# Sparse attention of the second block: norms, angle tables and key rotation issued between the input product's tiles, index scores and attention queries reordered

## The chip, the cores and the metric

One core of one Trainium2 chip runs the whole program in one launch. The metric is the device time of one execution in microseconds (us). TensorE does matrix products and transposes (PE, and PEld for its weight loads), VectorE (DVE) and ScalarE (ACT) do element work, GpSimd (POOL) does element work and issues some DMAs, SyncE (SP) issues the large weight loads.

## The reference, cut to what matters

Two models of two layers each run one after the other on 256 tokens of width 2048. The change lies in the first layer of the second model. There one product `h = xn @ even_w_in` gives all inputs of a sparse attention (`dsa_mixer`) and of a recurrent mixer (`rwkv7_mixer`), which shifts its part by one token and blends it.

```python
def dsa_mixer(h, cos_a, sin_a, cos_i, sin_i, cq_norm, ckv_norm, kidx_norm, w_uq, w_uk, w_uv, w_qidx):
    c_q, c_kv, k_rope, k_idx, w_idx = split_cols(h, [512, 256, 32, 64, 16])
    c_q = rms_norm(c_q, cq_norm)
    c_kv = rms_norm(c_kv, ckv_norm)
    k_rope = apply_partial_rope(k_rope, cos_a, sin_a, 32)
    q = einsum('bsr,rhd->bshd', c_q, w_uq)                 # 8 heads of 128
    q_rope = apply_partial_rope(q[..., :32], ...)
    q_lat = einsum('bshd,rhd->bshr', q[..., 32:], w_uk)
    q_idx = apply_partial_rope(einsum('bsr,rhd->bshd', c_q, w_qidx), ...)   # 16 heads of 64
    k_idx = apply_partial_rope(rms_norm(k_idx, kidx_norm), ...)
    # per block of 128 queries:
    score = einsum('bqh,bqhs->bqs', w_idx, relu(q_idx . k_idx))
    sel = top_k(where(allowed, score, -inf), 64)
    # softmax of (q_lat . c_kv + q_rope . k_rope) over the selected keys, times c_kv, times w_uv
hm = h + (token_shift(h) - h) * mu                         # rwkv7_mixer's columns
```

## The kernel before, in words

**Products.** A weight slab of 2 MB is loaded into a ring of three by SyncE (L258 to L273). Every tile (128 output channels) of a product takes half of one. ScalarE rounds the tile's weights to fp32r in two halves (`act_feed`, L295), VectorE subtracts to get the remainder of the first half (`dve_feed`, L311), GpSimd that of the second half (`pool_feed`, L329). `pe_tile` (L336) then runs 16 pairs of matmuls, L349 and L350. VectorE adds the tile's two halves out of PSUM (L362) and multiplies by the norm (L559). Pieces of a tile go into one of two buffers, so a tile's feed may begin when the tile two before it is done, and `ahead` lets every engine feed one tile ahead.

**The input product** (`pe_evin`, `act_evin`, `dve_evin`) has 35 tiles, n = 0 to 34. Tiles 0 to 7 are the sparse attention's own (`cq`, `ckv`, `kid`, `kro`, the last with the index weights in it). Tiles 8 to 34 belong to the recurrent mixer: after sum and norm VectorE makes three more instructions on each, L1618 (times mu), L1620 (subtract) and L1622 (add the shifted row). In rounds 1 to 16 VectorE also scales one block of the residual stream (L1603). VectorE's order in a round is: feed the next tile, L1603, sum and norm of tile n, L1618, L1620, L1622. ScalarE in a round only feeds.

**The sparse attention** (`pe_dsa`, `act_dsa`, `dve_dsa`, `pool_dsa`) starts when tile 34 is done. In order: GpSimd loads the constants (L1636, L1637); VectorE computes two angle tables, with ScalarE's sines (L1651 to L1677); TensorE turns the index weights (L1723); three norms one after the other, each of squares (L437, L447), a sum by TensorE (L1711), a root (L439), a reciprocal (L449) and a product (L482); the rotation of the two keys (TensorE L1690, VectorE L1697, L1698, L1700); a transpose of `ckv` (L1736); eight tiles of index queries and then eight of attention queries (L1748, copied out by ScalarE L1865), each rotated; eight index products (L1764) with two ReLUs each (ScalarE L1872) and 32 accumulations (VectorE L1920); the selection `dve_select` (L1936), first all of the first 128 queries, then all of the others; and a loop of 13 rounds over the eight heads (L1767 to L1806): latent queries L1778, scores L1790 and L1791, masking and maximum (L625, L628, L630), exponential (L642), share (L650, L652), transpose (L1816), values (L1829), output (L1805) and copy (L1933). GpSimd's loads for the recurrent mixer come behind: L1997 and L1998 after tile 34, L2001 after the last scores. The recurrent mixer waits for the last head.

**What orders it.** There is no planner for this part. Every engine has its list of instructions written out by hand, and waits on counting semaphores: `K.dve.of(key)` is the count at which the instruction recorded under that key is done. `K.dve.now()` is the count of the instruction just before, so that wait makes an instruction wait for its predecessor. PSUM banks are taken in turn.

## Time and profile before

| | |
|---|---|
| runs shown | 4569.15, 4564.98, 4549.57 us; median 4564.98 |
| the profiled execution | 4556.82 us, of which 4555.5 us span |
| mean granted TensorE clock | 0.931 |
| PE, DVE, ACT, POOL busy | 91%, 61%, 40%, 34% |

The profiled execution lies between the runs. Its span is from the first to the last instruction; 1.3 us lie around it. All times in the rows below are us from the start of the span.

### The profile page before, as it was taken

To read this page: it belongs to the slowest core of one execution; us is meant where nothing else is said; L and a number is where in the kernel's file an instruction comes from. 1 tells how busy PE (TensorE), PEld (TensorE's weight loads), DVE (VectorE), ACT (ScalarE), POOL (GpSimd) and SP (SyncE) were. 2 spreads that over 40 slices of the span, in tenths; PEclk is the share of its full clock that TensorE was granted. 3 is DMA by queue.
4 is the path that set the end of the run, shared out by engine and by line. 5 is a ranking of instruction groups with operands and counts; after the bars stand their busy time and mean duration, and the time that the engine had idled before them with its cause. 6 is when DMAs were issued, how large, how long until landed. Compare 5 with 4: busy or idle time off the path is not lost.

```text
span 4555.5 us, 58299 instructions
## 1 busy us (share of the span) xinstructions
PE 4151.7 (91%) x24034; PEld 3456.0 (76%) x24034; DVE 2778.9 (61%) x4036; ACT 1819.2 (40%) x2818; POOL 1526.8 (34%) x710
## 2 busy tenths in 40 slices
PE   5898999999999857877899999999799998999998
PEld 3786887778788745666677888888676887888887
DVE  0436635863688865554768464468997577554557
ACT  1435434543553323211444343344364454343334
POOL 0332432333234300000333444444465442444443
PEclk8999999999999978777899999999876999999999
DMA  8653665345444400000444554555200543545543
GB/s 362 259 208 135 251 247 190 145 178 222 167 148 166 181 19 15 1 1 1 167 165 169 185 189 183 196 189 186 111 1 27 198 183 130 187 183 187 196 180 139
DMA packets 53481, 711.35 MB, mean 156 GB/s; under 512 B 5952, under 2 KB 8128, under 8 KB 10848
## 3 DMA queue, kind: packets, MB, share of 16 engines
q1 hardware_dynamic: 47664, 684.15, 40.1%
q0 software_dynamic: 3488, 21.37, 1.3%
q8 instruction: 190, 3.11, 0.3%
q10 hardware_dynamic: 2064, 2.10, 0.1%
q14 instruction: 75, 0.61, 0.0%
HBM read 705.50 MB, written 2.10 MB: 155 GB/s over the span
## 4 chain that ended last, share of the span: by engine, by line
PE 73%; DVE 18%; ACT 4%; DMA 2%; issue 2%; POOL 0%; DVEq 0%; ACTq 0%; POOLq 0%; SPq 0%
PE ps L349 37%; PE ps L350 19%; DVE pieces L311 3%; DMA ring<-in_ada 2%; PE ps L758 2%; ACT pieces L295 1%; PE ps L2198 1%; DVE r L1139 1%; DVE opb L538 1%; PE ps L2992 1%; DVE scr L503 1%; PE ps L2993 1%; DVE opa L538 1%; PE ps L1748 1%; PE ps L2222 1%
## 5 line engine op out<-in xcount | busy, mean ns | idle before, releaser
L349 PE MATMUL ps<-opa,pieces 128*128 128x512 f32 x6192 | 2245.8, 406 | 73.7 <-DVE pieces L311 48.4
L329 POOL TENSOR_TENSOR pieces<-ring,pieces 128x1024 fp32r<-128x1024 f32 x539 | 1356.4, 2517 | 2617.3 <-ACT pieces L295 2581.6
L350 PE MATMUL ps<-opa,pieces 128*128 128x256 f32 x6192 | 1740.2, 281 | 0.0
L295 ACT ACTIVATE pieces<-ring 128x1024 fp32r<-128x1024 f32 (+1 forms) x1110 | 1098.6, 1036 | 919.6 <-PE ps L350 912.9
L349 PEld LDWEIGHTS ps<-opa,pieces 128*128 128x128 f32 x6192 | 1171.0, 189 | 373.1 <-issue 64.3
L350 PEld LDWEIGHTS ps<-opa,pieces 128*128 128x128 f32 x6192 | 1177.2, 190 | 8.0 <-issue 4.8
L349 PE MATMUL ps<-opb,pieces 128*128 128x512 f32 x2560 | 910.4, 397 | 24.1 <-DVE pieces L311 19.6
L311 DVE TENSOR_TENSOR pieces<-ring,pieces 128x1024 fp32r<-128x1024 f32 (+1 forms) x571 | 732.4, 1283 | 263.3 <-ACT pieces L295 261.4
L350 PE MATMUL ps<-opb,pieces 128*128 128x256 f32 x2560 | 726.4, 284 | 0.0
L349 PEld LDWEIGHTS ps<-opb,pieces 128*128 128x128 f32 x2560 | 483.8, 189 | 144.9 <-DVE x L391 20.2
L350 PEld LDWEIGHTS ps<-opb,pieces 128*128 128x128 f32 x2560 | 484.3, 189 | 0.1
L389 DVE TENSOR_TENSOR x<-ps,x 128x256 f32<-128x256 f32 x192 | 81.2, 423 | 319.0 <-PE ps L350 319.0
L362 DVE TENSOR_REDUCE scr<-ps 128x256 f32<-128x512 f32 x203 | 140.1, 690 | 177.1 <-PE ps L350 176.7
L408 ACT ACTIVATE opb<-scr 128x256 fp32r<-128x256 f32 x129 | 53.9, 418 | 445.2 <-DVE scr L2715 444.7
L503 DVE TENSOR_TENSOR scr<-scr 128x256 f32<-128x256 f32 x195 | 140.8, 737 | 18.5 <-ACT scr L494 15.1
L559 DVE TENSOR_TENSOR scr<-scr,rstd 128x256 f32<-128x256 f32 x136 | 125.6, 924 | 4.6
L758 PE MATMUL ps<-ring,ada 128*32 128x256 f32 x1536 | 105.6, 422 | 24.9 <-DMA ring<-in_ada 24.9
L362 DVE TENSOR_REDUCE m<-ps 128x256 f32<-128x512 f32 x48 | 33.2, 691 | 112.6 <-PE ps L350 112.6
L758 PEld LDWEIGHTS ps<-ring,ada 128*32 128x32 f32 x1536 | 48.5, 118 | 65.6 <-DMA ring<-in_ada 26.7
L413 DVE TENSOR_TENSOR opb<-scr,opb 128x256 fp32r<-128x256 f32 x129 | 54.9, 425 | 62.5 <-ACT opb L408 62.5
L391 DVE TENSOR_TENSOR x<-ps,x 128x256 f32<-128x256 f32 x192 | 81.5, 424 | 6.6
L1032 ACT ACTIVATE scr<-m 128x256 f32<-128x256 f32 x48 | 20.0, 418 | 162.1 <-DVE m L362 162.1
(467 smaller groups left out, 4222.3 us busy)
## 6 DMA issues: line engine op xcount, KB each, us to landing
ring<-in_up SPq DMA_DIRECT2D x64, 2048.0 KB, 7.8
ring<-in_down SPq DMA_DIRECT2D x64, 2048.0 KB, 7.8
ring<-in_win SPq DMA_DIRECT2D x56, 2048.0 KB, 8.2
ring<-in_ada SPq DMA_DIRECT2D x48, 2048.0 KB, 12.1
ring<-in_wout SPq DMA_DIRECT2D x24, 2048.0 KB, 8.1
ring<-in_evin SPq DMA_DIRECT2D x18, 2048.0 KB, 7.9
ring<-in_evout SPq DMA_DIRECT2D x8, 2048.0 KB, 7.9
ring<-in_xkv SPq DMA_DIRECT2D x8, 2048.0 KB, 7.9
```

The costliest lines, as they stand in the source:

```text
L295: a.do.activation(K.parts_of(p)[0][:, s, :], w[:, s, :], ACT.Copy).then_inc(*K.hi.up((p, h)))
L311: v.do.tensor_tensor(lo[:, s, :], w[:, s, :], hi[:, s, :].bitcast(F), ALU.subtract).then_inc(*K.lo.up(p))
L329: g.do.tensor_tensor(lo[:, s, :], w[:, s, :], hi[:, s, :].bitcast(F), ALU.subtract).then_inc(*K.lo2.up(p))
L349: pe.do.matmul(b[:, 0:512], hi[:, k, :], op[:, 512 * k:512 * k + 512], start=i == 0, stop=False)
L350: t = pe.do.matmul(b[:, 0:256], lo[:, k, :], half(op, 0, k), start=False, stop=i == kt - 1)
L362: return K.v.do.tensor_reduce(out, b, AX.X, ALU.add)
L389: v.do.tensor_tensor(x, b[:, 0:256], x, ALU.add).then_inc(*K.dve.up())
L391: v.do.tensor_tensor(x, b[:, 256:512], x, ALU.add).then_inc(*K.dve.up(key))
L503: v.do.tensor_tensor(K.acc[z], K.acc[z], K.sqr[z][k % 2], ALU.add).then_inc(*K.dve.up((*key, "acc", k)))
L538: K.v.do.scalar_tensor_tensor(out=half(op, 1, k), in0=src, scalar=gain, in1=half(op, 0, k).bitcast(F), op0=ALU.mult, op1=ALU.subtract).the ...
L559: return v.do.tensor_tensor(out, out, rstd[0:out.shape[0]], ALU.mult)
L758: t = pe.do.matmul(b[q:q + 32, 0:256], K.sc[:, 2 * k:2 * k + 32], w[:, k, :], start=k < 4, stop=k >= 12)
```

## The change

It does these things:

1. `act_evin` and `dve_evin`: for tiles 8 to 34, L1618 and L1620 are replaced by one ScalarE instruction, tile times (1 - mu), one round later, and VectorE's shifted add (before L1622) follows a round later too, after the next feed. Two small instructions make `omu` = 1 - mu.
2. New functions `pe_dsa_ahead`, `act_dsa_ahead`, `dve_dsa_ahead` are called once in every round. They issue the three norms (rounds 8 to 17), the turn of the index weights (19, 20), the angle tables (19 to 29) and the two key rotations (30 to 33).
3. `pool_dsa` goes in front of the feeds of tiles 18 to 34, waits for the last L1603, and issues three DMAs in place of two. The constants lie in the upper half of the `mix` buffer.
4. `pe_dsa` and the others: index queries, their rotation, index products and scores run in one loop of 11 rounds. The attention queries come behind it, which on TensorE is while VectorE selects. Their rotation is done two heads ahead inside the loop over heads.
5. `dve_select` takes its steps for both query blocks in turn, and waits for the same block's step before, no longer for the instruction just before.

```diff
 def act_evin(K):
-    for n in range(35):
-        act_feed(K, ahead(K, p + n))
+    for n in range(36):
+        if n < 35:
+            act_feed(K, ahead(K, p + n))
...
+        if n > 8:
+            d, h, mu, om = shifted(K, n - 1)
+            a.wait_ge(*K.dve.of(("evn", n - 1)))
+            a.do.activation(d, h, ACT.Identity, scale=om).then_inc(*K.act.up(("evd", n - 1)))
+        act_dsa_ahead(K, n)
 def dve_evin(K):
+    for a, w, name in ((0, 24, "mu"), (24, 3, "mul")):
+        v.do.tensor_scalar(K.omu[:, a:a + w], K.col(name), -1.0, 1.0, ALU.mult, ALU.add).then_inc(*K.dve.up())
...
+        if n > 8:
+            d, h, mu, om = shifted(K, n - 1)
+            v.wait_ge(*K.act.of(("evd", n - 1)))
+            v.do.scalar_tensor_tensor(out=d[:, 1:256], in0=h[:, 0:255], scalar=mu, in1=d[:, 1:256], op0=ALU.mult,
+                                      op1=ALU.add).then_inc(*K.dve.up(("ev", n - 1)))
+        dve_dsa_ahead(K, n)
...
-        v.do.tensor_scalar(d, h, mu, None, ALU.mult).then_inc(*K.dve.up())
-        v.do.tensor_tensor(d, h, d, ALU.subtract).then_inc(*K.dve.up())
-        v.do.scalar_tensor_tensor(out=d[:, 1:256], in0=h[:, 0:255], scalar=mu, in1=d[:, 1:256], op0=ALU.mult,
-                                  op1=ALU.add).then_inc(*K.dve.up(("ev", n)))
+            d = shifted(K, n)[1]
+            if n > 9:
+                v.wait_ge(*K.dve.of(("ev", n - 2)))
+        dve_normed(K, p + n, d, K.rr, ("evs", n)).then_inc(*K.dve.up(("evn", n)))
 def pool_dsa(K):
-    g.wait_ge(*K.tile.of(K.first["evin"] + 34))
-    g.do.dma_start(K.dc, K.D["dsac"]).then_inc(*K.load["dsac"].up("dsac", 16))
+    g.wait_ge(*K.dve.of(("nf", "y", 15)))
+    g.do.dma_start(K.iota, K.D["dsac"][:, 0:256]).then_inc(*K.load["io5"].up("iota", 16))
+    g.do.dma_start(K.dc, K.D["dsac"][:, 256:1028]).then_inc(*K.load["dsac"].up("dsac", 16))
     g.do.dma_start(K.sfi[:, 0:1].bitcast(I32), K.D["sf"]).then_inc(*K.load["sf"].up("sf", 16))
+def pe_dsa_ahead(K, n):
+    if n in (9, 11, 13):
+        i = (n - 9) // 2
+        key, src, _, _ = dsa_norms(K)[i]
...
+        pe.wait_ge(*K.act.of((key, "sq")))
+        for k in range(len(src)):
+            t = pe.do.matmul(b[:, 0:256], K.ones, K.sqd[k], start=k == 0, stop=k == len(src) - 1)
+    if n == 19:
...
+            t = pe.do.transpose(b[:, P * i:P * i + P], K.kro[:, P * i:P * i + P], K.ident)
+    if n in (30, 31):
...
+        pe.do.matmul(b[:, 0:256], perm, buf, start=True, stop=True).then_inc(*K.prod.up(key))
+def act_dsa_ahead(K, n):
+    if n in (10, 12, 14):
+        a.do.activation(K.rsd[i], K.bank[key][:, 0:256], ACT.Sqrt, bias=K.eps[1e-5], scale=1.0 / width).then_inc(*K.act.up((key, "std")))
+    if n in (8, 10, 12):
+        for k, x in enumerate(src):
+            a.do.activation(K.sqd[k], x, ACT.Square).then_inc(*K.act.up((key, "sq")))
+    if n == 20:
+        a.do.activation(K.wix, ...)
+        a.do.activation(K.kro, K.kro, ACT.Copy, scale=K.inv[:, 2:3]).then_inc(*K.act.up("kro"))
+    if n in (23, 28):
+        a.do.activation(dsa_tables(K)[2 * i + 1], K.an, ACT.Sin).then_inc(*K.act.up())
+        a.do.activation(K.turns, K.an, ACT.Sin, scale=0.5).then_inc(*K.act.up(("sine", i)))
+def dve_dsa_ahead(K, n):
+    if n in (11, 14, 16):
+        v.do.reciprocal(K.rsd[i], K.rsd[i]).then_inc(*K.dve.up((dsa_norms(K)[i][0], "rstd")))
+    if n in (12, 13, 15, 17):
+        for k in ks:
+            v.do.scalar_tensor_tensor(out=src[k], in0=src[k], scalar=gain(k), in1=K.rsd[i], ...)
...
+    # angle tables: the eleven instructions of each, one or two a round, from rounds 19 and 24
+    if n in (32, 33):
+        v.do.tensor_tensor(an, K.bank[key][:, 0:256], sin, ALU.mult).then_inc(*K.dve.up((*key, "sin")))
+        v.do.tensor_tensor(buf, buf, cos, ALU.mult).then_inc(*K.dve.up())
+        v.wait_ge(*K.dve.now())
+        v.do.tensor_tensor(buf, buf, an, ALU.add).then_inc(*K.dve.up((*key, "done")))
 def pe_dsa(K):
     pe.wait_ge(*K.dve.of(("ev", 34)))
+    pe.wait_ge(*K.dve.of(("rkr", "done")))
...
+    for n in range(11):
+        if n < 8:
+            pe_dsa_queries(K, "qidx", n)
+        if 0 <= n - 1 < 8:
+            pe_rope2(K, ("r", "qidx", n - 1), K.permI, K.qi[:, n - 1, :], K.act, ("qidx", n - 1))
+        if 0 <= n - 3 < 8:
+            pe_dsa_index(K, n - 3)
+    for n in range(8):
+        pe_dsa_queries(K, "uq", n)
+    for n in range(2):
+        uq_rope(n)
...
+        if i + 2 < 8:
+            uq_rope(i + 2)
 def dve_dsa(K):
+    for n in range(11):
+        if n < 8:
+            dve_rope2(K, ("r", "qidx", n), K.qi[:, n, :], cosI, sinI, n)
+        for m in range(2 * n - 6, 2 * n - 4) if n >= 3 else ():
+            v.wait_ge(*K.act.of(("idx", m // 2, m % 2)))
+            v.wait_ge(*K.dve.now())
+            for qt in range(2):
+                v.do.scalar_tensor_tensor(out=K.SC[:, qt, :], ...).then_inc(*K.dve.up(("score", m)))
     dve_select(K)
+    for n in range(2):
+        uq_rope(n)
...
+        if i + 2 < 8:
+            uq_rope(i + 2)
 def pool_program(K):
     pool_block1(K)
+    pool_feed(K, K.first["evin"] + 17)
+    pool_dsa(K)
     pool_feed(K, K.first["evin"] + 34)
-    pool_dsa(K)
```

## Rows read from the trace of the kernel before

**Rows 1.** The page: busy time of the engines, and shares of the chain that ended last.
```profile
PE 4151.7 (91%) x24034; PEld 3456.0 (76%) x24034; DVE 2778.9 (61%) x4036; ACT 1819.2 (40%) x2818; POOL 1526.8 (34%) x710
...
PE 73%; DVE 18%; ACT 4%; DMA 2%; issue 2%; POOL 0%; DVEq 0%; ACTq 0%; POOLq 0%; SPq 0%
```
**Rows 2.** Windows: stretch, its length, busy us (instructions) by engine, granted clock, DMA.
```profile
1387.60:1420.90 33.30, 33.30 (x194) 29.36 (x193) 29.13 (x25) 12.09 (x13) 14.87 (x6) 1.00 0.43 163
1420.90:1475.60 54.70, 52.39 (x288) 43.63 (x286) 53.17 (x63) 18.05 (x19) 22.89 (x9) 1.00 0.51 189
1475.60:1577.10 101.50, 98.29 (x544) 82.94 (x544) 93.14 (x103) 33.43 (x33) 40.27 (x16) 1.00 0.51 187
1577.10:1612.00 34.90, 10.20 (x23) 6.49 (x24) 19.49 (x40) 6.07 (x14) 2.14 (x4) 0.53 0.17 53
1612.00:1648.00 36.00, 35.92 (x163) 30.74 (x161) 18.28 (x48) 6.74 (x17) 0.00 (x0) 0.98 0.16 59
...
1668.20:1691.50 23.30, 0.00 (x0) 0.00 (x0) 21.62 (x69) 0.00 (x0) 0.00 (x0) 0.50 0.00 0
1691.50:1744.70 53.20, 51.98 (x248) 45.10 (x248) 26.81 (x88) 24.52 (x66) 0.54 (x1) 0.96 0.08 30
```
**Rows 3.** Timeline of VectorE and GpSimd in the input product: start, us, instruction.
```profile
1416.39 1.22 DVE L311 TENSOR_TENSOR pieces<-ring,pieces 128x1024 fp32r<-128x1024 f32 x1
1417.41 2.48 POOL L329 TENSOR_TENSOR pieces<-ring,pieces 128x1024 fp32r<-128x1024 f32 x1 [2.98 <-ACT pieces L295]
1417.52 2.64 DVE L1603 SCALAR_TENSOR_TENSOR x<-x,cols,rstd 128x256 f32<-128x256 f32 x1
...
1477.16 0.42 DVE L1620 TENSOR_TENSOR even<-scr,even 128x256 f32<-128x256 f32 x1
1477.62 0.48 DVE L1622 SCALAR_TENSOR_TENSOR even<-scr,cols,even 128x255 f32<-128x255 f32 x1
1477.74 2.62 POOL L329 TENSOR_TENSOR pieces<-ring,pieces 128x1024 fp32r<-128x1024 f32 x1 [3.53 <-ACT pieces L295]
1478.02 3.42 DVE L311 TENSOR_TENSOR pieces<-ring,pieces 128x1024 fp32r<-128x1024 f32 x1
```
**Rows 4.** Timeline behind the last tile: sum of tile 34, constants, norms.
```profile
1577.07 0.68 DVE L362 TENSOR_REDUCE scr<-ps 32x256 f32<-32x512 f32 x1 [3.63 <-PE ps L350]
1577.33 0.55 POOL L1636 DMA_DIRECT2D dsa<-in_dsac  x1 [7.41 <-PE ps L350]
1579.05 0.47 DVE L1622 SCALAR_TENSOR_TENSOR even<-scr,cols,even 32x255 f32<-32x255 f32 x1
1602.20 1.75 DVE L449 RECIPROCAL rstd<-rstd 128x256 f32<-128x256 f32 x1 [2.78 <-ACT rstd L439]
```
**Rows 5.** Timeline of the queries, index products and scores.
```profile
1612.25 4.20 PE L1748 MATMUL ps<-even,ring 128*128 128x256 f32 x16
1618.87 1.89 PE L1748 MATMUL ps<-even,ring 128*128 128x256 f32 x8
1619.07 0.42 DVE L1697 TENSOR_TENSOR dsa<-ps,dsa 128x256 f32<-128x256 f32 x1 [0.94 <-PE ps L1690]
1619.42 0.41 DVE L1698 TENSOR_TENSOR dsa<-dsa 128x256 f32<-128x256 f32 x1
1619.87 0.42 DVE L1700 TENSOR_TENSOR dsa<-dsa 128x256 f32<-128x256 f32 x1
1621.03 1.89 PE L1748 MATMUL ps<-even,ring 128*128 128x256 f32 x8
1648.08 5.55 PE L1764 MATMUL ps<-even,dsa 64*128 64x256 f32 x48
1650.56 17.64 DVE L1920 SCALAR_TENSOR_TENSOR dsa<-scr,dsa 128x256 f32<-128x256 f32 x32
```
**Rows 6.** Timeline of the first heads.
```profile
1691.51 1.09 ACT L1881 ACTIVATE dsa<-ps 128x512 f32<-128x512 f32 x2 [26.00 <-DVE dsa L1967]
1692.25 2.05 PE L1790 MATMUL ps<-even,dsa 128*128 128x256 f32 x4 [32.06 <-ACT dsa L1881]
```

More of the change, by code:

```diff
@@ L1700, in dve_rope2, with pe_dsa_queries, pe_dsa_index @@
     v.do.tensor_tensor(buf, buf, t, ALU.add).then_inc(*K.dve.up((*key, "done")))
[L1703 removed]
+def pe_dsa_queries(K, name, n):
     pe = K.pe
[L1706 to L1712 removed]
+    ap, landed = K.slab_at(K.raw[name])
+    w = r3(ap, 4)
+    pe.wait_ge(*landed)
+    pe.wait_ge(*K.dve.of(("ncq", "y", 3)))
+    b, was = K.wide.take(K.act, (name, n))
+    K.bank[name, n] = b
+    pe.wait_ge(*was)
+    for k in range(4):
+        t = pe.do.matmul(b[:, 0:256], w[:, k, P * n:P * n + P], K.cq[:, k, :], start=k == 0, stop=k == 3)
+    t.then_inc(*K.prod.up(("slab", name) if n == 7 else (name, n)))
+def pe_dsa_index(K, i):
+    pe = K.pe
+    pe.wait_ge(*K.dve.of(("r", "qidx", i, "done")))
+    pe.wait_ge(*K.dve.of(("rki", "done")))
+    bb = []
+    for par in range(2):
+        b, was = K.wide.take(K.act, ("idx", i, par))
+        K.bank["idx", i, par] = b
+        pe.wait_ge(*was)
+        bb.append(b)
+    for par in range(2):
+        for qt in range(2):
+            t = pe.do.matmul(bb[par][:, 256 * qt:256 * qt + 256], K.qi[64 * par:64 * par + 64, i, qt * P:qt * P + P],
+                             K.kid[64 * par:64 * par + 64, :], start=True, stop=True)
+    t.then_inc(*K.prod.up(("idx", i)))
 def pe_dsa(K):
@@ L1787, in pe_dsa @@
                 pe.wait_ge(*K.act.of(("lat", n)))
-                pe.wait_ge(*K.dve.of(("rkr", "done")))
                 for c in range(2):
@@ new lines, in dve_select, with of, at, done @@
+    v = K.v
+    def of(qt):
+        return K.SC[:, qt, :], K.m8[:, qt, :], *(K.scr[:, 1536 + 1024 * qt + 256 * i:1792 + 1024 * qt + 256 * i] for i in range(4))
+    def at(key, qt):
+        v.wait_ge(*K.dve.of(("sel", key, qt)))
+    def done(t, key, qt):
+        t.then_inc(*K.dve.up(("sel", key, qt)))
+    both = range(2)
+    v.wait_ge(*K.dve.now())
+    for qt in both:
+        sc, m8, w, gt, eq, cum = of(qt)
+        done(v.do.tensor_tensor(sc, sc, K.allow[:, qt, :], ALU.add), "sum", qt)
@@ new lines, in dve_select @@
+    for qt in both:
+        sc, m8, w, gt, eq, cum = of(qt)
+        at("sum", qt)
+        done(v.do.tensor_copy(w, sc), ("w", 0), qt)
+    for r in range(8):
+        for qt in both:
+            sc, m8, w, gt, eq, cum = of(qt)
+            at(("w", r), qt)
+            done(v.do.max(m8[:, 0:8], w), ("m", r), qt)
+        for qt in both if r < 7 else ():
+            sc, m8, w, gt, eq, cum = of(qt)
+            at(("m", r), qt)
+            done(v.do.match_replace(w, m8[:, 0:8], w, -3.3e38), ("w", r + 1), qt)
@@ new lines, in dve_select @@
+    for qt in both:
+        sc, m8, w, gt, eq, cum = of(qt)
+        th = m8[:, 7:8]
+        at(("m", 7), qt)
+        done(v.do.tensor_scalar(gt, sc, th, 0.0, ALU.is_gt, ALU.add, accum_out=m8[:, 8:9]), "gt", qt)
+        done(v.do.tensor_scalar(eq, sc, th, None, ALU.is_equal), "eq", qt)
+        done(v.do.memset(w, 1.0), "one", qt)
+    for qt in both:
+        sc, m8, w, gt, eq, cum = of(qt)
+        at("one", qt)
+        done(v.do.tensor_tensor_scan(cum, w, eq, 0.0, ALU.mult, ALU.add), "cum", qt)
+        done(v.do.tensor_scalar(m8[:, 9:10], m8[:, 8:9], -1.0, 64.0, ALU.mult, ALU.add), "left", qt)
@@ new lines, in dve_select @@
+    for qt in both:
+        sc, m8, w, gt, eq, cum = of(qt)
+        at("left", qt)
+        done(v.do.tensor_scalar(cum, cum, m8[:, 9:10], None, ALU.is_le), "le", qt)
+    for qt in both:
+        sc, m8, w, gt, eq, cum = of(qt)
+        at("le", qt)
+        done(v.do.tensor_tensor(eq, eq, cum, ALU.mult), "take", qt)
+    for qt in both:
+        sc, m8, w, gt, eq, cum = of(qt)
+        at("take", qt)
+        done(v.do.tensor_tensor(gt, gt, eq, ALU.add), "all", qt)
+    for qt in both:
+        sc, m8, w, gt, eq, cum = of(qt)
+        at("all", qt)
```

288 lines of the change are left out of this document (119 added, 169 removed).

## The prediction

> **What bounds it now.** I read the page first. TensorE is busy for 91% of the span and carries 73% of the chain that ended last, VectorE 18% [rows 1]. So only stretches in which TensorE stands still, or works in small pieces behind a chain, can give much. The windows show where they lie [rows 2]. In the input product TensorE is busy nearly throughout at full clock (98.3 of 101.5 us in its last 17 tiles). Then come 34.9 us with 10.2 us of its work at a granted clock of 0.53, most of it at the lower level of 1.2 GHz: the constants, tables, norms and key rotations. Queries, rotations and index products fill it again until 1648, but then it waits for scores, and for the selection's 23.3 us it does nothing. The loop over heads is TensorE's own (52.0 of 53.2 us).
>
> **1. The work in front of the first query.** Tile 34's sum starts at 1577.07 and the first query matmul at 1612.25: 35.2 us [rows 4, 5]. After the change, what is left there is tile 34's own tail. Today it ends with L1622 at 1579.05 + 0.47 = 1579.5 [rows 4]; ScalarE takes over one of its steps and VectorE loses two, which I put at no difference. Behind it TensorE has the transposes of `ckv`, four of about 0.26 us (estimate from the 0.216 us of a query's record, below), say 1.1 us with starting up: the first query at 1580.6, 3.5 us behind the sum. **Gain 31.7 us.** The clock before that point was full and the pause is 2.2 us; the pauses of the 34.9 us window are longer, so whether it drops here no row says. If the first queries run at 1.2 GHz, 1.7 us more each: 0 to 4 us, I take 0.
>
> **2. Index queries and scores.** Today queries, index products and scores follow each other, 1612.25 to 1668.20 = 56.0 us. In the new loop a steady round has on TensorE four query matmuls and a rotation, 2.16 us (1618.87 to 1621.03), and an index product, 5.55/48 x 8 records = 0.93 us: 3.1 us [rows 5]. VectorE has a rotation, from 1619.07 to 1619.87 + 0.42 = 1.22 us, and four accumulations; today's 32 take 17.64 us, 0.55 each, since every one waits for the one before. The new ones wait once per pair. A pair without a wait starts 0.35 us apart (1619.07, 1619.42), one with it 0.45 (1619.42, 1619.87); so a pair of 0.48 us instructions takes about 0.93 and the round 1.22 + 1.86 = 3.1 us [rows 5]. ScalarE has a copy and two ReLUs, under 1.7 us by L1881's 1.09 for two of the same width [rows 6]. So the round is 3.1 us with the two engines level. TensorE's rounds 0 to 2 take 1.73 + 2 x 2.16, round 3 takes 3.1, and rotation 3 is 2.16 into round 4: 1591.9. From there VectorE has five rounds of 3.1 and three of 1.86: 1613.0. The stretch 1580.6 to 1613.0 is 32.4 us. **Gain 23.6 us.** If the two engines wait for each other in every round, 8 x 1 us are lost: bounds 15 to 25.
>
> The eight attention queries (8 x 1.73 us = 13.8, at 0.216 a record [rows 5]) lie behind it on TensorE beside the selection, which idles TensorE for 23.3 us [rows 2]: nothing. Without that cover they would cost their 13.8.
>
> **3. The selection.** It is 23.3 us of VectorE alone [rows 2]. Every instruction waits for its predecessor now; in the new order the predecessor is of the other block, and some 23 waits of each block are met when the instruction comes up. By the two spacings of [rows 5] each saves 0.1 us: 46 x 0.1 = 4.6, **gain 4.6 us**, to 18.7. The row shows a start before the end of the one ahead; the Trainium skill ("VectorE: DVE Perf Modes", The DRAIN you can't avoid) states that the next instruction does not start until the pipe is empty, and that leaving semaphores out saves nothing. By the skill the selection would stay at 23.3 and the sum below be 4.6 us smaller. Bounds 0 to 5.5; I go by the row, though it is of other instructions than the selection's.
>
> **4. The heads.** Today the first two latent products are done before the mask is: ScalarE copies at 1691.51 and scores begin at 1692.25 [rows 6]. After the change VectorE rotates head 0 first (1.2 us), TensorE makes latent 0, rotation 2, latent 1 and rotation 3 (0.86 + 0.43, twice, = 2.6), at a low clock at first after its idle, which today's first four score matmuls pay as well (2.05 us in place of 0.86 [rows 6]). Scores start 4.2 us later in the low-clock case, of which the 1.5 us paid there is not paid again: 2.7. Rotations 4 to 7 add 4 x 0.43 = 1.7 us to a loop that TensorE bounds; VectorE is busy 26.8 of 53.2 there, so 1.2 us more in six rounds fit [rows 2]. **Loss 4.4 us**, bounds 2 to 10.
>
> **5. The input product.** A tile takes 5.55 us where VectorE has spare time (33.3 for six), 6.08 in tiles 8 to 16 (54.7 for nine), 5.97 after (101.5 for 17) [rows 2]. The reason is in [rows 3]. L1603 begins while GpSimd's L329 runs and ends with it, 2.64 in place of some 0.47 us; where the feed L311 comes behind L1622 it meets L329 instead, 3.42 in place of 1.22, and the next tile waits for its pieces. The Trainium skill says why ("SBUF — State Buffer", Who interferes with whom): instructions with two SBUF inputs lock out, or are locked out by, GpSimd's for their whole length; the trace agrees. After the change the feed comes before L329 in every round, as in 1416.39, and it is the shifted add that is held, when no tile waits for it. Tiles 17 to 33 then go at 5.55: 17 x 5.55 = 94.3, plus TensorE's added turn and two rotations (about 1.4) and 1 us for rounds in which angle instructions push the feed: 96.8 against 101.5, gain 4.7. Tiles 8 to 16 are full. VectorE has sum 0.7, norm 0.45, feed 1.15, L1603 and add 0.45 each, and one hold of 2.15: 5.4 a tile, and the norms add three reciprocals of 1.75 [rows 4] and seven products of 0.46 over them = 8.5. That is 57 against 54.7: loss 2. TensorE's 14 added records for the sums (3.0) fit into that loss, ScalarE's 27 scalings of 0.42 and its few others stand beside 16 to 18 busy of 54.7. **Gain 2.7 us**, bounds -6 to 8.
>
> **6. Queues.** On GpSimd the three loads, 0.55 us each [rows 4], now stand before the feed of tile 18, behind a wait for the last L1603. That ends with L329 of round 16, some 5 us after a tile's end; the loads end at 6.7, and ScalarE hands over the next pieces only 2.3 us after the tile's next end, at 7.9. Nothing. The loads' landing, on the path today, is in part 1. SyncE gets no new load; it frees the index query slab earlier. The recurrent mixer's load L2001 keeps its place before the last heads.
>
> **Sum.** 31.7 + 23.6 + 4.6 - 4.4 + 2.7 = 58.2 us. The profiled execution took 4556.8 us, so 4498.6; the runs' median lies 8 us higher. I say 4500.
>
> **The rivals.** (a) VectorE stays the input product's bound. Its added 8.5 us of norms and some 9 us of tables and rotations push the feed behind L329 again and again, and tiles keep 5.97 to 6.1 us while TensorE's 4.4 us come on top. For it: VectorE is busy 53.2 of 54.7 us in tiles 8 to 16 [rows 2]. Against it: it loses two instructions, some 0.85 us, a tile. Part 5 is then -5: gain 50, 4507. (b) Rounds of the index loop and of the heads are bound by handovers rather than by an engine: part 2 is 15, part 4 is -9: gain 44, 4513. (c) The selection does not speed up: its instructions wait for an empty pipe whichever block they belong to, against the 0.35 us of [rows 5], which are not its own instructions. Gain 53.6, 4503. That is the Trainium skill's rule of part 3. (d) Slower. In the rounds of the norms TensorE waits for ScalarE's squares and roots, which wait for VectorE's backlog; with repeated pauses its clock falls to 1.2 GHz within the input product, and a tile takes 11.1 us in place of 5.55. It decides from about 10 such tiles on, whose 55.5 us eat the gain; 15 of them are 83 us, a loss of 25 in all: 4582. Against it: the squares are issued a round or more ahead of their sum, and the present waits of 0.3 to 0.5 us a tile leave the clock at 1.00 [rows 2]. (e) The reordering does not take effect, since the attention queries or the constants turn out to be awaited somewhere in front; the likeliest place is the heads, and half the gain goes: 4530.
>
> **Chances.** The forecast 0.58, (a) 0.15, (b) 0.10, (c) 0.10, (d) 0.02, (e) 0.05. About 0.5%, 23 us, is what a measurement of this kernel can tell from no change. The range takes the forecast with its bounds (up to 67 us of gain, from the lower runs) and (a) to (c) with the scatter of the runs above: 4481 to 4526. Faster by over 0.5%: 0.94; within: 0.04; slower: 0.02.
>
> **What would show it.** From the sum of tile 34 to the first query 3 to 4 us, no standstill of TensorE over 3 us before the selection, accumulations in pairs, the last one some 36 us behind that sum; selection 18 to 19 us with starts 0.35 us apart; first scores about 5 us behind the mask; heads 57 us; tiles 17 to 33 at 5.6 us with L311 at 1.2 us and L1622's successor at 2.6. I am wrong if rounds of the index loop take over 3.5 us, if L311 still shows 3.4 us from tile 18 on, or if TensorE's clock falls before tile 34.

## The result, and the profile after

The changed kernel takes **4497.16 us** (median of 4 runs, 4489.91 to 4501.4) against 4566.94 us of the kernel before in the same rounds: ratio 0.9855, 95% interval 0.9835 to 0.9876, a gain of 57 to 75 us. Its profiled execution took 4493.5 us, 5.1 us under the 4498.6 that the sum gave for it.

The page after: busy time by engine, and the chain that ended last.

```profile
PE 4131.8 (92%) x24034; PEld 3441.7 (77%) x24034; DVE 2739.7 (61%) x3981; ACT 1828.3 (41%) x2847; POOL 1521.9 (34%) x711
...
PE 76%; DVE 15%; ACT 4%; DMA 2%; issue 2%; POOL 0%; DVEq 0%; ACTq 0%; SPq 0%; POOLq 0%
```

TensorE has 76% of the chain in place of 73% and VectorE 15% in place of 18% [rows 1]. Where that came from is in the windows after, with the same columns as [rows 2]: tiles 8 to 16; tiles 17 to 33; sum of tile 34 to the first query; to the last score; to the mask; the heads; the recurrent mixer's stretch behind them.

```profile
1421.30:1476.70 55.40, 54.71 (x305) 46.86 (x304) 52.71 (x54) 25.09 (x34) 24.70 (x12) 1.00 0.52 191
1476.70:1573.20 96.50, 96.46 (x549) 83.78 (x547) 86.28 (x94) 41.45 (x56) 41.90 (x16) 1.00 0.54 200
1573.20:1575.90 2.70, 0.47 (x4) 0.48 (x5) 2.04 (x4) 0.51 (x1) 1.09 (x2) 1.00 0.51 141
1575.90:1611.60 35.70, 34.83 (x175) 27.20 (x174) 23.06 (x56) 14.04 (x28) 0.00 (x0) 0.95 0.22 84
1611.60:1629.00 17.40, 8.69 (x41) 7.31 (x39) 17.36 (x70) 1.92 (x5) 0.00 (x0) 0.86 0.00 0
1629.00:1688.00 59.00, 56.84 (x268) 48.99 (x268) 35.71 (x114) 24.21 (x66) 0.53 (x1) 0.95 0.08 27
1688.00:2076.60 388.60, 292.92 (x1743) 225.02 (x1744) 211.59 (x371) 76.93 (x147) 0.00 (x0) 0.79 0.00 1
```

The stages of four profiles side by side, in us ("again": the two kernels run once more, unedited). A stage runs from the start of one instruction to the start of another in its own trace. The marks are the sums (L362) of tiles 8, 17 and 34, the first weight load of a query, the last accumulation of the scores, the last instruction of the mask, the last head's copy, and the last matmul of L2198 (L2315 after). So "tiles 8 to 16" and "tiles 17 to 33" name the rounds by the sums that they begin with; in them TensorE works on tiles 9 to 17 and 18 to 34.

| stage | before | before, again | after | after, again | gain |
|---|---|---|---|---|---|
| tiles 8 to 16 | 54.7 | 54.8 | 55.4 | 55.4 | -0.7 |
| tiles 17 to 33 | 101.5 | 101.3 | 96.5 | 95.3 | 5.0, 6.0 |
| sum of tile 34 to first query | 34.9 | 34.5 | 2.6 | 2.6 | 32.3, 31.9 |
| first query to last score | 55.7 | 55.6 | 35.8 | 34.1 | 19.9, 21.5 |
| selection, to the mask | 23.4 | 23.4 | 17.4 | 17.4 | 6.0 |
| heads, to the last head's copy | 53.2 | 53.1 | 59.0 | 60.1 | -5.8, -7.0 |
| recurrent mixer behind it | 403.5 | 393.3 | 388.6 | 400.1 | 14.9, -6.8 |

From the sum of tile 8 to the last head's copy that is 323.4 and 322.6 us before, 266.7 and 264.9 after: **a gain of 56.7 and 57.7, where the sum said 58.2.** The spans differ by more, 4555.5 to 4491.8 = 63.7 us. The other 7 lie in stages that the change doesn't touch: the recurrent mixer gained 14.9, the stretch from the first to the last of L2992 (L3109 after) lost 8.0 (226.9 to 234.9), the rest is within 2.

The product after: VectorE and GpSimd in round 17, in the columns of [rows 3].

```profile
1500.51 0.43 DVE L559 TENSOR_TENSOR scr<-scr 128x256 f32<-128x256 f32 x1
1500.85 1.22 DVE L311 TENSOR_TENSOR pieces<-ring,pieces 128x1024 fp32r<-128x1024 f32 x1
1501.42 2.91 POOL L329 TENSOR_TENSOR pieces<-ring,pieces 128x1024 fp32r<-128x1024 f32 x1 [2.75 <-ACT pieces L295]
1501.98 2.62 DVE L1632 SCALAR_TENSOR_TENSOR even<-scr,cols,even 128x255 f32<-128x255 f32 x1
...
1454.40 3.42 DVE L311 TENSOR_TENSOR pieces<-ring,pieces 128x1024 fp32r<-128x1024 f32 x1
...
1460.98 1.89 DVE L559 TENSOR_TENSOR scr<-scr 128x256 f32<-128x256 f32 x1
```

As forecast, the feed (L311) starts before GpSimd's L329 and takes 1.22 us, and the deferred shifted add L1632 stands the hold (2.62). The last two lines are from the rounds of the norms: there the feed still takes 3.42 us, or the norm L559 is held. Between the sums of tiles 8 and 34, 12 feeds of the kernel before take 3.4 us; after the change 2 do in the first profile and none in the second. What TensorE's waits for the feed came to over these tiles (us in total, times, longest), first after, then before:

```profile
PE ps L349 <- DVE pieces L311: 0.6, 2, 0.3
```
```profile
PE ps L349 <- DVE pieces L311: 5.4, 17, 0.6
```

Behind tile 34, after:

```profile
1573.20 0.68 DVE L362 TENSOR_REDUCE scr<-ps 32x256 f32<-32x512 f32 x1 [2.85 <-PE ps L350]
...
1575.43 0.66 PE L1849 MATMUL ps<-io,even 128*128 128x128 f32 x4 [2.27 <-DVE even L1632]
1575.92 5.30 PE L1817 MATMUL ps<-even,ring 128*128 128x256 f32 x16
...
1589.33 0.74 PEld L1834 LDWEIGHTS ps<-even,dsa 64*128 64x128 f32 x8 [0.33 <-issue]
1590.40 1.59 PEld L1817 LDWEIGHTS ps<-even,ring 128*128 128x128 f32 x8 [0.33 <-issue]
...
1593.83 1.99 PE L1817 MATMUL ps<-even,ring 128*128 128x256 f32 x8
1594.19 1.87 DVE L2005 SCALAR_TENSOR_TENSOR dsa<-scr,dsa 128x256 f32<-128x256 f32 x4
1595.66 0.59 PE L1793 MATMUL ps<-dsa,mix 128*128 128x256 f32 x2
1596.18 1.14 PE L1834 MATMUL ps<-even,dsa 64*128 64x256 f32 x8
1597.26 1.99 PE L1817 MATMUL ps<-even,ring 128*128 128x256 f32 x8
```

In place of the 34.9 us window with TensorE at a clock of 0.53 there is a pause of 2.3 us. A round of the index loop takes 1597.26 - 1593.83 = 3.43 us, all of it TensorE's: 1.83 queries, 0.52 rotation, 1.08 index product.

The selection after, on VectorE, and the start of the heads:

```profile
1613.20 0.75 DVE L2052 MAX8 dsa<-scr 128x8 f32<-128x256 f32 x2
...
1613.93 0.41 DVE L2056 MATCH_REPLACE8 scr<-dsa,scr 128x256 f32<-128x256 f32 x1
...
1614.32 0.41 DVE L2056 MATCH_REPLACE8 scr<-dsa,scr 128x256 f32<-128x256 f32 x1
1614.65 0.74 DVE L2052 MAX8 dsa<-scr 128x8 f32<-128x256 f32 x2
...
1628.79 0.50 DVE L2084 TENSOR_SCALAR dsa<-scr 128x256 f32<-128x256 f32 x2
1630.76 2.04 PE L1874 MATMUL ps<-dsa,ring 128*128 128x256 f32 x4 [10.46 <-DVE dsa L1803]
1633.45 1.50 PE L1874 MATMUL ps<-dsa,ring 128*128 128x256 f32 x4
1635.21 1.03 PE L1887 MATMUL ps<-even,dsa 128*128 128x256 f32 x4
```

The mask is done at 1629.29 and the first scores start at 1635.21, 5.9 us behind it; before, the mask was done at 1691.41 and they started 0.8 behind it [rows 6].

### The profile page after: what moved, and what is told of

It reads as the page before. It is cut to its first block, busy times and chain, and to the rows that moved or that the text cites. A ratio compares the mean times of both kernels' runs of the same rounds, so it can differ in the third digit from the quotient of the medians.

```text
span 4491.8 us, 58254 instructions
## 1 busy us (share of the span) xinstructions
PE 4131.8 (92%) x24034; PEld 3441.7 (77%) x24034; DVE 2739.7 (61%) x3981; ACT 1828.3 (41%) x2847; POOL 1521.9 (34%) x711
## 4 chain that ended last, share of the span: by engine, by line
PE 76%; DVE 15%; ACT 4%; DMA 2%; issue 2%; POOL 0%; DVEq 0%; ACTq 0%; SPq 0%; POOLq 0%
PE ps L349 40%; PE ps L350 20%; DVE pieces L311 2%; DMA ring<-in_ada 2%; PE ps L758 2%; ACT pieces L295 1%; PE ps L2315 1%; DVE r L1139 1%; PE ps L3109 1%; PE ps L3110 1%; DVE opa L538 1%; PE ps L2339 1%; PE ps L2332 1%; PE ps L3132 1%; PE ps L3133 1%
## 5 line engine op out<-in xcount | busy, mean ns | idle before, releaser
L329 POOL TENSOR_TENSOR pieces<-ring,pieces 128x1024 fp32r<-128x1024 f32 x539 | 1351.6, 2508 | 2601.7 <-ACT pieces L295 2556.3
L349 PE MATMUL ps<-opb,pieces 128*128 128x512 f32 x2560 | 909.9, 397 | 25.3 <-DVE pieces L311 19.6
L311 DVE TENSOR_TENSOR pieces<-ring,pieces 128x1024 fp32r<-128x1024 f32 (+1 forms) x571 | 707.5, 1239 | 265.0 <-ACT pieces L295 262.5
L362 DVE TENSOR_REDUCE scr<-ps 128x256 f32<-128x512 f32 x203 | 139.8, 689 | 186.3 <-PE ps L350 186.0
L559 DVE TENSOR_TENSOR scr<-scr,rstd 128x256 f32<-128x256 f32 x136 | 120.8, 888 | 4.6
L362 DVE TENSOR_REDUCE m<-ps 128x256 f32<-128x512 f32 x48 | 33.2, 691 | 111.6 <-PE ps L350 111.6
L413 DVE TENSOR_TENSOR opb<-scr,opb 128x256 fp32r<-128x256 f32 x129 | 54.8, 425 | 62.5 <-ACT opb L408 62.5
```

The source lines that it names most:

```text
L311: v.do.tensor_tensor(lo[:, s, :], w[:, s, :], hi[:, s, :].bitcast(F), ALU.subtract).then_inc(*K.lo.up(p))
L329: g.do.tensor_tensor(lo[:, s, :], w[:, s, :], hi[:, s, :].bitcast(F), ALU.subtract).then_inc(*K.lo2.up(p))
L349: pe.do.matmul(b[:, 0:512], hi[:, k, :], op[:, 512 * k:512 * k + 512], start=i == 0, stop=False)
L362: return K.v.do.tensor_reduce(out, b, AX.X, ALU.add)
L413: K.v.do.tensor_tensor(part(op, 1, k, src), src, part(op, 0, k, src).bitcast(F), ALU.subtract).then_inc(*K.dve.up((*opkey, k)))
L559: return v.do.tensor_tensor(out, out, rstd[0:out.shape[0]], ALU.mult)
```

## The experiments

All of them compute the whole reference. Stages are read as in the table above. The changed kernel has two profiles there; every edited version has one, so its stages are single measurements.

**1 and 2. The two kernels again, unedited.**

> The kernel before once more, for its profile. In the two profiles at hand the change gives 56.3 us up to the last head's copy, and 7.4 us more come from stages whose code is the same: the recurrent mixer is 14 us shorter after the change, the S5 stage 7 us longer, both with another mean granted clock. Theory 1 (these stages vary from run to run by the granted clock): here the stretch from the last head's copy to the last matmul of the triangular inverses is not 403.5 us again but anywhere from 385 to 410, and the S5 stage anywhere from 225 to 245. Theory 2 (the change shortens the recurrent mixer): 402 to 405 again. Everything up to the last head's copy: 1744.3 within 1 us by both.

> The changed kernel once more, for its profile. Theory 1 (varying clock): the recurrent stretch is anywhere from 385 to 410 us, not 388.6 again; theory 2 (the change does it): 387 to 390 again. Up to the last head's copy 1688.0 us within 1 us by both.

They took 4544.74 and 4502.46 us. The last head's copy came 5.4 and 1.3 us earlier than in the first profiles, where less than 1 us was expected; no stage of the change differs by more than 1.7 us. The recurrent mixer's window in three profiles, of before, of before again and of after again (length, busy time of PE, PEld, DVE, ACT, POOL, granted clock):

```profile
1744.30:2147.80 403.50, 309.10 (x1744) 237.84 (x1744) 211.75 (x371) 77.18 (x147) 0.00 (x0) 0.75 0.00 1
```
```profile
1738.90:2132.20 393.30, 297.55 (x1744) 228.92 (x1744) 211.67 (x371) 76.92 (x147) 0.00 (x0) 0.78 0.00 1
```
```profile
1686.70:2086.80 400.10, 305.48 (x1743) 235.23 (x1744) 211.74 (x371) 77.14 (x147) 0.00 (x0) 0.77 0.00 1
```

The kernel before alone gives 403.5 and 393.3, the changed one 388.6 and 400.1. VectorE's and ScalarE's busy time stay put; TensorE's goes with the granted clock, 309 us at 0.75 and 293 at 0.79. Over all thirteen profiles of the study this stretch lies between 388.6 and 403.5 whatever was edited. So the 7 us beyond the stages of the change are scatter of one kernel against itself, and from here on I read stages, not spans.

**3. The selection's two blocks in turn again, all else as changed.**

```diff
-    for r in range(8):
-        for qt in both:
-            at(("w", r), qt)
-            done(v.do.max(m8[:, 0:8], w), ("m", r), qt)
+    for qt in range(2):
+        for r in range(8):
+            v.wait_ge(*K.dve.now())
+            v.do.max(m8[:, 0:8], w).then_inc(*K.dve.up())
...
```

> The changed kernel with the selection of before: one query block after the other, each instruction waiting for its predecessor. Theory A (alternating blocks lets an instruction start before the end of the one ahead): the selection takes 23.2 us again in place of 17.2, and everything behind it comes 6.0 us later, since nothing on TensorE is bound there. Theory B (the selection got shorter for another reason, such as the four buffers of its own for the second block): 17 to 18 us, or clearly in between.

The run took 4514.48 us. The selection took 23.4 us, as before; every other stage of the table up to the heads stayed within 0.9 us of the changed kernel's second profile. Its VectorE rows:

```profile
1607.95 0.43 DVE L2038 MAX8 dsa<-scr 128x8 f32<-128x256 f32 x1
1608.41 0.09 DVE L2041 MATCH_VALUE_LOAD scr<-dsa,scr 128x8 f32 x1
...
1608.93 0.43 DVE L2038 MAX8 dsa<-scr 128x8 f32<-128x256 f32 x1
```

An instruction that waits for the one ahead starts 0.46 us behind it (1607.95 to 1608.41), a whole step takes 0.98 us for one block; in the changed kernel two MAX8 take 0.75 together and the step of both blocks 1613.20 to 1614.65 = 1.45 us, 0.73 a block. The order of the blocks is worth the whole 6.0 us. The edit also takes the second block's own buffers away; what speaks for the order is the spacing of these starts.

**4. The moved work behind the product.** The new tail of a tile stays, the norms, tables and key rotations come behind tile 34.

```diff
+    for n in range(36):
+        dve_dsa_ahead(K, n)
...
-        dve_dsa_ahead(K, n)
```

(and the same for TensorE's and ScalarE's parts, with a wait in front of the key rotations' products.)

> The changed kernel with the norms, tables and key rotation issued in one piece behind the input product's last tile, by the same functions; the constants are still loaded early, and the tiles keep their new tails (scaling on ScalarE, shifted add after the feed). Theory A (the work in front is on the path there and nearly free between the tiles): the product's 9 tiles from 8 on take 50 to 51 us, the next 17 94.5 to 95.5, so the product is 5 to 7 us shorter than in the changed kernel, and the path from tile 34's sum to the first query is about 28 to 33 us in place of 2.7. In all 20 to 26 us slower than the changed kernel. Theory B (part of that chain hides behind something else, so that moving it gave less than its length): less than 15 us slower.

4518.77 us median of 4 runs, ratio 0.9898 (0.9855 to 0.9941). Its windows: tiles 8 to 16, tiles 17 to 33, and from there to the first query.

```profile
1419.50:1469.00 49.50, 49.50 (x288) 43.26 (x287) 47.09 (x45) 21.65 (x27) 23.21 (x13) 1.00 0.54 194
1469.00:1565.00 96.00, 96.00 (x555) 83.72 (x554) 79.30 (x68) 39.02 (x49) 40.32 (x17) 1.00 0.56 210
1565.20:1591.80 26.60, 9.19 (x23) 5.73 (x24) 19.14 (x39) 7.38 (x18) 1.09 (x2) 0.58 0.13 48
```

By the markers the product takes 49.9 + 94.3 = 144.2 us, that is 26 tiles of 5.55, with TensorE busy in every microsecond of the windows. Two things come apart here. The new tail alone gives 156.2 - 144.2 = **12.0 us**. The moved work costs the product 151.9 or 150.7 less 144.2 = 7.7 or 6.5 us and saves 26.6 - 2.6 = 24.0 behind it: **about 17 us net.** From the sum of tile 8 to the last head's copy this kernel takes 283.8, the changed one 266.7 and 264.9, so 17 to 19 less; the expectation was 20 to 26.

**5. The old tail with the moved work.** VectorE does the scaling, the subtraction and the shifted add in the tile's own round again.

```diff
-            a.do.activation(d, h, ACT.Identity, scale=om).then_inc(*K.act.up(("evd", n - 1)))
...
+            v.do.tensor_scalar(d, h, mu, None, ALU.mult).then_inc(*K.dve.up())
+            v.wait_ge(*K.dve.now())
+            v.do.tensor_tensor(d, h, d, ALU.subtract).then_inc(*K.dve.up())
+            v.wait_ge(*K.dve.now())
+            v.do.scalar_tensor_tensor(out=d[:, 1:256], in0=h[:, 0:255], scalar=mu, in1=d[:, 1:256], ...)
```

> The changed kernel with the tail of a recurrent tile as before: three VectorE instructions after sum and norm, all in front of the next feed; norms, tables and key rotations still between the tiles. Theory A (what lets the tiles take more work is that the feed now comes before GpSimd's instruction, and two instructions are gone): the feeds L311 are held again and the work that was put between the tiles is no longer free. Tiles 8 to 16: 54.7 + 8.5 = 63 us, tiles 17 to 33: 101.4 + some 9 to 11 = 111 us; t17 to t34 at least 107. Theory B (VectorE had the time anyway, the tail is a small matter): 56 to 58 and 101 to 103. Behind tile 34 as in the changed kernel, 114 to 115 us.

4511.84 us. Its two windows of the product, then VectorE's rows of one round:

```profile
1417.70:1478.10 60.40, 54.95 (x303) 46.45 (x302) 58.33 (x73) 21.83 (x26) 23.61 (x12) 1.00 0.48 179
1478.10:1583.90 105.80, 99.78 (x550) 83.63 (x549) 99.34 (x127) 33.45 (x38) 39.78 (x16) 1.00 0.48 179
```
```profile
1452.18 2.26 DVE L559 TENSOR_TENSOR scr<-scr 128x256 f32<-128x256 f32 x1
...
1455.72 1.22 DVE L311 TENSOR_TENSOR pieces<-ring,pieces 128x1024 fp32r<-128x1024 f32 x1
```

The product takes 60.4 + 105.9 = 166.3 us: 10 more than before the change. Moving the work in without the new tail would have cost 10; with the work there, the tail is worth 166.3 less 151.9 or 150.7 = 14 to 16 us. Both windows lie between the two theories (63 and 111 us, or 56 to 58 and 101 to 103). Six feeds take 3.4 us here. The rows show what happens in a round where the feed is not held: the hold falls on L559, the scaling, subtraction and shifted add come behind it (left out above, 0.35 to 0.48 us each), and the feed starts 1455.72 - 1452.18 = 3.54 us behind L559, against 0.34 in the changed kernel. TensorE waits for the feed 15 times, 11.3 us in all.

**6. The index loop in turn.** Queries and rotations for all eight heads, then eight index products; the attention queries stay behind them. VectorE and ScalarE take their parts in the same order.

```diff
-    for n in range(11):
+    for n in range(9):
         if n < 8:
             pe_dsa_queries(K, "qidx", n)
...
-        if 0 <= n - 3 < 8:
-            pe_dsa_index(K, n - 3)
+    for n in range(8):
+        pe_dsa_index(K, n)
```

> The changed kernel with index queries, index products and scores in turn: eight query tiles with rotations, then the eight products with their scores; attention queries still beside the selection, accumulations still waiting once per pair. From the first query to the last score now: 34.1 to 35.8 us, of which TensorE's rounds of 3.43. Theory A (the loop hides TensorE's queries beside VectorE's scores): queries 17.3 + 1.5, scores 16 x 0.97 = 15.5 and 1.5 us in between, 35.5 to 36.5 in all, so the loop itself gives only 1 to 2 us, and most of the 20 us between before and after comes from taking the eight attention queries (17.3 us) out of the path. Theory B (the overlap is what pays): 42 us or more.

4492.64 us; first query to last score 34.9 us. The pipelined loop gives 34.1 where its first queries run at full clock, as they do here (see part 2 below): interleaving is worth 0.8 us. The 32 accumulations, now in one block, take 15.63 us, 0.49 each, where before they took 0.55 [rows 5].

**7. The same, with the attention queries in front of the index products.**

```diff
+    for n in range(8):
+        pe_dsa_queries(K, "uq", n)
     for n in range(8):
         pe_dsa_index(K, n)
-    for n in range(8):
-        pe_dsa_queries(K, "uq", n)
```

> The kernel of index_in_turn, with the eight attention queries in front of the index products on TensorE and their copies there on ScalarE; their rotations stay in the loop over heads. Theory A (the selection covers TensorE's 13.8 us for nothing, and taking them off the path is what made query to last score shorter): query to last score 34.9 + 12 to 14 = 47 to 49 us, selection and heads as before (17.3, 59 to 60). Theory B (they overlap with VectorE's rotations or scores in any order): 41 or less.

4508.84 us; first query to last score 48.6, 13.7 more than in run 6, the other stages up to the heads within 0.2. TensorE's row of them:

```profile
1590.72 13.98 PE L1817 MATMUL ps<-even,ring 128*128 128x256 f32 x64
```

The attention queries cost their 13.8 us in the path and nothing beside the selection.

**8. A wait before every accumulation**, in place of one for each pair.

```diff
-            v.wait_ge(*K.dve.now())
             for qt in range(2):
+                v.wait_ge(*K.dve.now())
```

> The changed kernel with every accumulation waiting for the one before, not once per pair. If the waits cost what the starts in the profiles say (about 0.1 us for each of 16 pairs), the eight rounds with a rotation have VectorE at 3.3 to 3.5 us beside TensorE's 3.43 and hide it, and the last rounds show it: query to last score 0.5 to 2 us more than the changed kernel's 34.1 to 35.8. If the round's bound is VectorE rather than TensorE: 2 us or more.

4505.71 us; first query to last score 35.8. The changed kernel's first profile has 35.8 as well, but there the first 16 query records took 5.30 us; here they took 3.62, and with those the changed loop needs 34.1. VectorE's last accumulations in this run, and in the second profile of the changed kernel:

```profile
1596.94 2.11 DVE L2005 SCALAR_TENSOR_TENSOR dsa<-scr,dsa 128x256 f32<-128x256 f32 x4
1600.47 8.77 DVE L2005 SCALAR_TENSOR_TENSOR dsa<-scr,dsa 128x256 f32<-128x256 f32 x16
```
```profile
1598.64 1.86 DVE L2005 SCALAR_TENSOR_TENSOR dsa<-scr,dsa 128x256 f32<-128x256 f32 x4
1601.92 7.77 DVE L2005 SCALAR_TENSOR_TENSOR dsa<-scr,dsa 128x256 f32<-128x256 f32 x16
```

Four take 0.25 us more, the last sixteen 1.0. The last round stretches from 3.28 (1598.64 to 1601.92) to 3.53 (1596.94 to 1600.47) and the ones ahead of it from 3.43 to 3.53 or more, since VectorE now bounds them: the waits saved are worth 1.7 us.

**9. The norms nine rounds later**, in the rounds in which VectorE was thought to have time.

```diff
-    if n in (11, 14, 16):
-        i = {11: 0, 14: 1, 16: 2}[n]
+    if n in (20, 22, 24):
+        i = {20: 0, 22: 1, 24: 2}[n]
```

(the sums, squares, roots and products move with them, the products one a round, up to round 29.)

> The changed kernel with the three norms nine rounds later (rounds 17 to 29 in place of 8 to 17), where VectorE no longer scales the residual stream. With no such work the tiles took 49.9 (8 to 16) and 94.3 us (17 to 33). Theory A (tiles 8 to 16 are bound by VectorE and GpSimd's shared time, later ones by TensorE): 8 to 16 fall from 55.4 to 50 or 51, 17 to 33 rise from 95.3 by TensorE's 3.0 us of sums and under 1.5 us more, to 98.3 to 100; together 1 to 2.5 us less than 150.8. Theory B (VectorE is short in the later rounds too): together the same or more.

4494.3 us. Tiles 8 to 16 take 49.9, but tiles 17 to 33 103.3: 153.2 together, 1.3 and 2.5 us more than the changed kernel, where 1 to 2.5 less was expected. Rows of VectorE, GpSimd and TensorE in one late round:

```profile
1512.32 1.74 DVE L1737 RECIPROCAL scr<-scr 128x256 f32<-128x256 f32 x1
...
1514.16 2.42 POOL L329 TENSOR_TENSOR pieces<-ring,pieces 128x1024 fp32r<-128x1024 f32 x1 [2.05 <-ACT pieces L295]
1514.37 2.36 DVE L1771 TENSOR_SCALAR mix<-scr 128x256 f32<-128x256 f32 x1
...
1518.49 1.22 DVE L311 TENSOR_TENSOR pieces<-ring,pieces 128x1024 fp32r<-128x1024 f32 x1
...
1519.85 0.76 PE L349 MATMUL ps<-opa,pieces 128*128 128x512 f32 x1 [2.32 <-DVE pieces L311]
```

A held shifted add (2.41 us from 1509.98), a reciprocal and a table instruction held behind L329 come one after the other here, and the feed behind them is late: TensorE stands still for 2.32 us. Behind that pause its granted clock is 0.70 from 1520 to 1525, with 21 matmuls in those 5 us against 31 in the next 5, some 1.6 us more by that count (estimate). Without this one round the 153.2 us would be about 149.3, 1.4 to 2.6 less than the changed kernel, as expected. The one feed that meets L329 in the late rounds (3.43 us at 1490.23) costs nothing: TensorE is busy in all 9 us of 1488 to 1497. So this profile does not show that the later rounds have no time to spare; it shows that norms and tables in one round can collide. Whether another execution has the same stall is not known.

**10 and 11. A version with the rest of the reasoning in it:** attention queries 0 and 1 and their rotations in the last rounds of the index loop, before the selection; score waits per block; the selection's first step reads the scores themselves, without the copy, and its row of ones is set once ahead.

```diff
+        if 8 <= n <= 9:
+            pe_dsa_queries(K, "uq", n - 8)
+        if 9 <= n:
+            uq_rope(n - 9)
...
-        done(v.do.tensor_copy(w, sc), ("w", 0), qt)
...
+            done(v.do.max(m8[:, 0:8], w if r else sc), ("m", r), qt)
```

> The changed kernel with four small edits: attention queries 0 and 1 and their rotations go in front of the selection (rounds 8 to 10 of the loop), scores wait for the same block's accumulation only, the first step of the selection reads the scores without a copy, and the row of ones is made once ahead. Expected by the theory that VectorE is the path from the last index query to the mask and TensorE behind it: query to last score 34.1 to 35.8 less 1 for the waits (the rotations, 2.5 us, come behind the last score's block in part); score to mask 17.4 less 0.9 plus up to 2.5; mask to last head 59.5 less 5 = 54.5. From tile 34 to the last head's copy 110 to 111 in place of 114.2 to 114.8. A rival: TensorE's order in rounds 8 and 9 delays the index products, and nothing is left of the gain.

> The kernel better, timed. By stages it is 3 us shorter than the changed kernel up to the last head (111.5 against 114.2 to 114.8 from tile 34's sum); the unchanged stages behind vary by more than that. Ratio to the kernel before 0.983 to 0.988, its interval not apart from the changed kernel's 0.9855.

4494.02 us in one run, 4503.04 us as the median of 6 others, ratio 0.9866 (0.9841 to 0.9891). Sum of tile 34 to last head's copy 111.5 and 110.1 us (110 to 111 expected), against 114.8 and 114.2: 3 to 5 us better where it was aimed. The first scores, in the timed version:

```profile
1624.61 2.04 PE L1889 MATMUL ps<-even,dsa 128*128 128x256 f32 x4 [7.59 <-ACT dsa L1981]
```

The mask is done at 1623.77, so they start 0.8 us behind it, as they did before the change. The ratio's interval overlaps that of the changed kernel (0.9835 to 0.9876): on the whole time the two can't be told apart, and I don't call this version faster.

## Why the prediction held, part by part

**1, work in front: 31.7 forecast, 32.3 and 31.9 measured.** The first query starts 2.7 us behind the sum of tile 34, with 3.5 forecast: the four transposes overlap the first queries' start (1575.43 to 1575.92). The open question was the clock. The first 16 query records took 5.30 us in one profile and 3.62 in the other, after pauses of 2.3 us both. The part allowed 0 to 4 us for that and took 0; it was 1.7 once and nothing once, and shows in the next stage.

**2, index queries and scores: 23.6 forecast, 19.9 and 21.5 measured.** The step that was mis-sized is the steady round: 3.1 us, with the two engines level. It is 3.43 us, TensorE's. Queries and rotation take 2.35 in place of the 2.16 read off before, and the index product 1.08 in place of 5.55/48 x 8 = 0.93. I had read both from rows in which TensorE does one kind of matmul for long; a round changes between 128-row and 64-row operands twice, and the weight loads show an idle of 0.33 us for it. Five such rounds make 5 x 0.33 = 1.7 us. Counted as the prediction counted, from the first query's matmul to the end of the last accumulation, the stretch at full clock is 34.5 us, 2.1 over the 32.4; the other 0.4 lie in the last sixteen accumulations, 7.77 us where 4 x 1.86 = 7.4 were counted. VectorE's side of a steady round, 1.22 + 1.87 = 3.09, was right. Runs 6 to 8 sort out what the 21.5 us (55.6 to 34.1) are made of: 13.7 the attention queries (run 7), some 3.4 their eight rotations of 0.43, 1.7 the waits (run 8), 0.8 the interleaving (run 6), together 19.6. Of the remaining 1.9, some 0.5 are the first 16 query records, which took 4.20 and 4.10 us in the kernel before and 3.62 here; the rest no run took apart. The prediction reads as if the pipelined rounds brought the gain. What brought most of it is that the attention queries left the path.

**3, the selection: 4.6 forecast, 6.0 measured.** I took 0.1 us for each of 46 waits from rows of other instructions. The selection's own rows give (0.98 - 0.73) / 2 = 0.125 us, and 46 x 0.125 = 5.8. Run 3 shows the order of the blocks as the cause. Rival (c) falls, and with it what the Trainium skill ("VectorE: DVE Perf Modes", The DRAIN you can't avoid) says of the next instruction, that it does not start until the pipe is empty, and of semaphores, that leaving them out saves nothing: by it the two orders would have had the same selection, and they have 17.4 and 23.4 us. The measurement decides. The same section adds that a next instruction that is not held starts earlier, which is what the rows of the changed kernel show.

**4, the heads: 4.4 lost by forecast, 5.8 and 7.0 measured.** The mechanism was right, the term for the start too small. In the prediction the 4.2 us have no full working (1.2 and 2.6 make 3.8), and the 1.5 us not paid again do not follow from its 2.05 and 0.86, which make 1.2. In the first profile scores start 5.9 us behind the mask where they started 0.8 behind it, 5.1 later against 4.2; the four matmuls of the first latent product come after an idle of 10.46 us and take 2.04 us, the rotation and latent 1 behind them 1.06 and 1.50, so the stretch of 2.6 became 1635.21 - 1630.76 = 4.45. The first scores then take 1.03 in place of 2.05, so 1.0 and not 1.5 comes back: 4.1 lost, and 5.8 with the 1.7 for rotations 4 to 7. In the second profile latent 1 takes 1.91 and the rotation behind it 1.06, scores start 6.7 us behind the mask and the first take 1.32: 5.9 later, 0.7 back and the 1.7 make 6.9 of the measured 7.0. Runs 10 and 11 show it from the other side: with two heads rotated before the selection the scores start 0.8 us behind the mask again, and the heads take 55.8 and 56.1.

**5, the input product: 2.7 forecast, 4.3 and 5.3 measured.** Both halves had the right sign: tiles 8 to 16 lost 0.7 (2 forecast), tiles 17 to 33 gained 5.0 and 6.0 (4.7). The mechanism is that of [rows 3]: GpSimd's L329 holds the instruction with two SBUF inputs that begins behind it, and in the new order the feed begins ahead of it; the Trainium skill's rule ("SBUF — State Buffer", Who interferes with whom) and the traces agree again, L559 held for 2.26 us in run 5 and L1632 for 2.62 in the changed kernel. The 5.55 us a tile is 144.2 / 26, met exactly in run 4. What the forecast of 2.7 hid is that it is a small difference of two large terms, 12.0 to 16 us for the tail against 6.5 to 10 for the work. I charged VectorE's 8.5 us of norms in full against tiles 8 to 16, but a held instruction counts as busy too: without the norms (run 4) the eight scalings of the residual stream take 21.1 us there, each held; with them they take 12.4, and VectorE's busy time rises by 5.6 us and not by 8.5 (47.1 to 52.7). Rival (a) was right in so far as two rounds of one profile still show L311 at 3.4 us; it was wrong in that they are few, and none comes from tile 18 on, which was to be the sign against the forecast: TensorE waited for the feed twice, 0.6 us in all. Run 9 bears on the spare time from tile 17 on, but one stall of some 4 us decides it.

**6, queues: nothing forecast.** GpSimd's three loads issue at 1470.55, 1471.10 and 1471.63, and its L329 follows at 1472.21. The longest that TensorE waits behind it is 0.27 us, for the feed at 1476.17. So 0.3 us at most; no run tested it by itself.

Rival (d) needed a low clock within the product; all windows of it in the changed kernel show 1.00. Run 9 shows what one stall does there, 2.3 us of pause and 5 us at 0.70, but it stayed the only one. Rival (e) falls, since each part took effect in its place. The nearness of 4500 to 4497.16 is partly luck: the parts' errors (+0.6, -3.7, +1.4, -1.4, +1.6 in the first pair of profiles) cancel to -1.5 us, and the recurrent mixer alone scatters by ten times that between executions. The 4500 was also taken from the profiled execution: from the runs' median, 4564.98, the same sum gives 4506.8. And rival (b)'s parts add up to 45.0 us of gain, where the prediction says 44.

## What to carry to other kernels

When an engine's queue is shared between a feed that others wait for and work that nobody waits for, put the feed ahead of the instruction of the other engine that will hold it, and let the hold fall on the slack work; test the order and the added load apart, since here +12 to +16 and -7 to -10 us showed as +4 to +5. Where every VectorE instruction depends on the one before, alternate two independent chains. Compare stages by markers when stages that weren't touched vary by more than the change you look for.
